# Odd tiles of the modulated norms finished by VectorE in two steps, with another order of work around the first projection and in the sparse attention

## What is computed

```python
def rms_norm(x, g):
    xf = x.astype(jnp.float32)
    y = xf * lax.rsqrt(jnp.mean(xf * xf, axis=-1, keepdims=True) + EPS)
    return (y * g.astype(jnp.float32)).astype(x.dtype)

def norm_modulate(h, g, shift, scale):
    return rms_norm(h, g) * (1 + scale) + shift
```

## Time and profile before

| | us |
|---|---|
| Three runs | 2070.64 (median), 2067.16, 2074.06 |
| The profiled execution, its own time | 2077.58 |
| Span of its instructions | 2075.7 |
| PE busy | 1947.7 (94%) |
| DVE busy | 1334.4 (64%) |
| ACT busy | 1073.5 (52%) |
| POOL busy | 280.0 (13%) |

### The profile page before, as it was taken

The page is one execution under the profiler, slowest core; times in us unless marked ns, Lnnn a source line. Parts: engine busy times, 40 slices in busy tenths (PEclk is TensorE's granted clock), DMA queues, the critical chain, the costliest instruction groups (busy, mean ns, idle before and its releaser), DMA issues.

```text
span 2075.7 us, 32710 instructions
## 1 busy us (share of the span) xinstructions
PE 1947.7 (94%) x13400; PEld 1659.5 (80%) x13400; DVE 1334.4 (64%) x2036; ACT 1073.5 (52%) x1744; POOL 280.0 (13%) x291
## 2 busy tenths in 40 slices
PE   6999889999999899899999889999988899999998
PEld 3675568888787785899998888999877688888886
DVE  2338545676545558677667556545666688888886
ACT  2346533333334466466555425444445577676774
POOL 1201123010100300332111412111101000000000
PEclk9999999999999899999999999999998999999998
DMA  8332443554222220245553113555542489889794
GB/s 320 127 137 103 163 175 109 183 183 183 110 85 90 88 102 21 89 177 183 203 184 141 43 38 121 200 183 203 202 165 72 177 326 341 324 319 349 303 346 164
DMA packets 52812, 364.81 MB, mean 176 GB/s; under 512 B 5936, under 2 KB 8240, under 8 KB 8880
## 3 DMA queue, kind: packets, MB, share of 16 engines
q1 hardware_dynamic: 50304, 359.68, 46.9%
q10 hardware_dynamic: 2352, 2.96, 0.5%
HBM read 361.57 MB, written 1.05 MB: 175 GB/s over the span
## 4 chain that ended last, share of the span: by engine, by line
PE 82%; DVE 8%; ACT 4%; issue 3%; POOL 2%; DMA 1%; SPq 0%; DVEq 0%; POOLq 0%; ACTq 0%
PE ps L77 22%; PE ps L78 21%; PE ps L79 21%; PE ps L74 15%; DVE WLO L91 3%; PE ps L82 2%; ACT R L85 2%; ACT WHI L85 1%; DVE SM L105 1%; POOL R L91 1%; DMA ring<-W 1%; DVE R L91 1%; POOL h L95 0%; DVE h L88 0%; DVE x L88 0%
## 5 line engine op out<-in xcount | busy, mean ns | idle before, releaser
L91 DVE TENSOR_TENSOR WLO<-ring,WHI 128x1024 fp32r<-128x1024 f32 x566 | 682.2, 1240 | 194.5 <-ACT WHI L85 193.9
L85 ACT ACTIVATE WHI<-ring 128x1024 fp32r<-128x1024 f32 x566 | 577.8, 1052 | 101.7 <-PE ps L79 98.0
L77 PE MATMUL ps<-HHI,WHI 128*128 128x256 f32 (+1 forms) x1584 | 514.4, 325 | 32.2 <-DVE HLO L88 18.0
L78 PE MATMUL ps<-HLO,WHI 128*128 128x256 f32 (+1 forms) x1648 | 526.1, 319 | 0.0
L79 PE MATMUL ps<-HHI,WLO 128*128 128x256 f32 (+1 forms) x1584 | 507.9, 321 | 0.0
L77 PEld LDWEIGHTS ps<-HHI,WHI 128*128 128x128 f32 x1584 | 305.1, 193 | 75.2 <-issue 29.0
L78 PEld LDWEIGHTS ps<-HLO,WHI 128*128 128x128 f32 x1648 | 316.1, 192 | 23.0
L79 PEld LDWEIGHTS ps<-HHI,WLO 128*128 128x128 f32 x1584 | 303.8, 192 | 24.3
L74 PE MATMUL ps<-R 64*64 64x64 f32 (+10 forms) x2448 | 192.7, 291 | 4.5 <-ACT R L85 2.5
L85 ACT ACTIVATE R<-ps,VEC 128x512 f32<-128x512 f32 (+1 forms) x106 | 69.3, 658 | 244.1 <-PE ps L79 242.0
L91 POOL TENSOR_TENSOR R<-R 128x256 f32<-128x256 f32 (+1 forms) x99 | 108.4, 1098 | 544.8 <-ACT R L85 543.6
(11 more groups left out here) (220 smaller groups left out, 2994.6 us busy)
## 6 DMA issues: line engine op xcount, KB each, us to landing
ring<-W SPq DMA_DIRECT2D x340, 1024.0 KB, 4.9
x<-xt SPq DMA_DIRECT2D x2, 1024.0 KB, 6.7
out<-x SPq DMA_DIRECT2D x2, 512.0 KB, 3.9
CR<-const_nsa ACTq DMA_DIRECT2D x1, 560.0 KB, 3.7
CR<-const_rw ACTq DMA_DIRECT2D x1, 448.0 KB, 3.4
CR<-const_gqa ACTq DMA_DIRECT2D x1, 320.0 KB, 10.3
CR<-const_mla ACTq DMA_DIRECT2D x1, 320.0 KB, 2.9
VEC<-vec ACTq DMA_DIRECT2D x1, 314.0 KB, 10.1
```

The source lines that it names most:

```text
L77: self.e.matmul(out, l[0], r[0], start=start, stop=False)
L78: self.e.matmul(out, l[0], r[1], start=False, stop=False)
L85: return self.e.activation(out, in_, func, **kw)
L91: return self.e.tensor_tensor(out, in0, in1, op)
```

## The change

In the modulated norms, for odd tiles, VectorE now writes x * rs into h, waits for that, and then finishes h * gain + shift in place. ScalarE's HHI of an odd tile is a plain copy and GpSimd has one subtraction left. Around norm 0 the two jobs, the weight units and the low part of tile 0 stand in another order: VectorE scales tile 0, subtracts unit 0, writes the low part of tile 0; unit 1 follows after tile 2, unit 2 after job 1, unit 3 after tile 5. TensorE does parts 0 to 2 of job 1 before k = 1, part 3 before k = 2 and the turn before k = 3. In the sparse attention ScalarE writes one WHI in each of rounds 2 to 5, between the exponentials and the copy, and the four subtractions for WLO are GpSimd's, by a new function. The diff in full:

```diff
--- before.py
+++ after.py
@@ -670,6 +670,14 @@
             e.tt(WLO[:, o:o + UNIT], src, WHI[:, o:o + UNIT], ALU.subtract).then_inc(
                 *did("w_lo", ("lo", u)))
 
+    def lo_units_pool(g, units):
+        for u in units:
+            c, col, _, _ = F.units[u]
+            o = (u % UNITS) * UNIT
+            g.wait_ge(*at("hi", u))
+            src = ring[:, (c % RING) * SLOT + col:(c % RING) * SLOT + col + UNIT]
+            g.tt(WLO[:, o:o + UNIT], src, WHI[:, o:o + UNIT], ALU.subtract).then_inc(*did("w_lo_pool", ("lo", u)))
+
     def split_of(p, o=0):
         return WHI[:, p.at:p.at + p.cn], WLO[:, p.at:p.at + p.cn]
 
@@ -873,7 +881,13 @@
         n = NORM[c]
         o, w = n["segs"][s]
         v.wait_ge(*at("rs", c))
-        v.stt(n["dst"](k)[:, o:o + w], n["src"](k)[:, o:o + w], n["gain"](k, s), bank("rs", c)[:, o:o + w],
+        d = n["dst"](k)[:, o:o + w]
+        if n["shift"] and not by_dve(c, k):
+            v.tt(d, n["src"](k)[:, o:o + w], bank("rs", c)[:, o:o + w], ALU.mult).then_inc(*did("normed"))
+            v.wait_ge(*last("normed"))
+            v.ts(d, d, n["gain"](k, s), n["shift"](k, s), ALU.mult, ALU.add).then_inc(*did("normed", ("nx", c, k, s)))
+            return
+        v.stt(d, n["src"](k)[:, o:o + w], n["gain"](k, s), bank("rs", c)[:, o:o + w],
               ALU.mult, ALU.mult).then_inc(*did("normed", ("nx", c, k, s)))
 
     def low_dve(v, c, k, s):
@@ -901,11 +915,14 @@
             if k < n["tiles"]:
                 for s in segs:
                     scale_dve(v, c, k, s)
-            if n["split"] and k >= 1 and by_dve(c, k - 1):
+            if n["split"] and k >= 1 and by_dve(c, k - 1) and (c or k > 1):
                 for s in segs:
                     low_dve(v, c, k - 1, s)
             if between:
                 between(k)
+            if (c, k) == (0, 0):
+                for s in segs:
+                    low_dve(v, c, 0, s)
 
     def apply_act(a, c, between=None):
         n = NORM[c]
@@ -913,7 +930,7 @@
             for s, (o, w) in enumerate(n["segs"]):
                 z = slice(n["t0"] + o, n["t0"] + o + w)
                 a.wait_ge(*at("nx", c, k, s))
-                if n["shift"]:
+                if n["shift"] and by_dve(c, k):
                     m = a.act(HHI[:, k, z], n["dst"](k)[:, o:o + w], ACT.Identity, bias=n["shift"](k, s))
                 else:
                     m = a.act(HHI[:, k, z], h[:, k, z], ACT.Copy)
@@ -929,10 +946,6 @@
             for s, (o, w) in enumerate(n["segs"]):
                 z = slice(n["t0"] + o, n["t0"] + o + w)
                 g.wait_ge(*at("nh", c, k, s))
-                if n["shift"]:
-                    d = n["dst"](k)[:, o:o + w]
-                    g.ts(d, d, n["shift"](k, s), None, ALU.add).then_inc(*did("pool_step"))
-                    g.wait_ge(*last("pool_step"))
                 g.tt(HLO[:, k, z], h[:, k, z], HHI[:, k, z], ALU.subtract).then_inc(*did("h_lo_pool", ("nl", c, k, s)))
 
 
@@ -1635,9 +1648,9 @@
     def gqa_pe(pe):
         st, steps = L["gqa_in"], L["ada0"]
         def second_job(k):
-            for s in {1: (0, 1), 2: (2,), 3: (3,)}.get(k, ()):
+            for s in {1: (0, 1, 2), 2: (3,)}.get(k, ()):
                 ada_part_pe(pe, L["ada_pe"][4 + s], 1, s)
-            if k == 4:
+            if k == 3:
                 ada_turn_pe(pe, 1)
                 give(bank_of["rs", 0])
 
@@ -3223,10 +3236,10 @@
 
     def nsa_act(a):
         for i in range(11):
-            if i == 6:
-                hi_units(a, L["o_out"].first)
             if 1 <= i < 8:
                 nsa_exp_act(a, i)
+            if 2 <= i < 6:
+                hi_units(a, L["o_out"].first[i - 2:i - 1])
             if 2 <= i < 10:
                 nsa_copy(a, i - 2, 1)
             if i >= 4 and i % 2 == 0:
@@ -3234,8 +3247,6 @@
 
     def nsa_dve(v):
         for i in range(1, 10):
-            if i == 7:
-                lo_units(v, L["o_out"].first)
             if i < 8:
                 nsa_max_dve(v, i)
             if 2 <= i <= 8:
@@ -3244,6 +3255,7 @@
                 nsa_copy(v, i - 2, 0)
 
     def nsa_pool(g):
+        lo_units_pool(g, L["o_out"].first)
         for f in range(4):
             g.wait_ge(*at("oh", f))
             g.tt(HLO[:, f, 0:256], h[:, f, 0:256], HHI[:, f, 0:256], ALU.subtract).then_inc(
@@ -3770,9 +3782,11 @@
         first_squares_act(a)
         root_act(a, 0)
         ada_row_act(a, 0, None)
-        hi_units(a, L["gqa_in"].first[0:2])
+        hi_units(a, L["gqa_in"].first[0:1])
 
         def second_job(k):
+            if k == 1:
+                hi_units(a, L["gqa_in"].first[1:2])
             if k == 3:
                 ada_row_act(a, 1, 0)
                 hi_units(a, L["gqa_in"].first[2:4])
@@ -3832,12 +3846,14 @@
         ada_job_dve(v, 0)
 
         def second_job(k):
+            if k in (0, 2):
+                lo_units(v, L["gqa_in"].first[k // 2:k // 2 + 1])
             if k == 3:
-                v.wait_ge(*at("mod0", 0, 0))
                 ada_job_dve(v, 1)
-                lo_units(v, L["gqa_in"].first[2:4])
+                lo_units(v, L["gqa_in"].first[2:3])
                 v.wait_ge(*at("mod", 0, 1))
-        lo_units(v, L["gqa_in"].first[0:2])
+            if k == 5:
+                lo_units(v, L["gqa_in"].first[3:4])
         apply_dve(v, 0, [("mod", 0, 0)], second_job)
         gqa_dve(v)
```

## The result

The changed kernel took 2061.74 us (median; 2054.73 to 2068.00) beside 2072.53 us (2065.68 to 2081.55) for the kernel before: a ratio of 0.9947, 95% interval 0.9935 to 0.9959, some 10.8 us less (8.5 to 13.5 by the interval). A second comparison (`b1_after`) gave 0.9962 (0.9948 to 0.9976), 7.9 us less (5.0 to 10.8). The forecast was 12.9 us less, 2057.7: within the first interval and outside the second.

The account below looks back on a forecast made before the run. TensorE, 82% of the chain of waits, bounds the kernel, so only its standstills can shrink: 5.1 + 0.8 + 3.4 - 0.2 + 3.8 = 12.9 us, from 2070.64 to 2057.7; range 2050 to 2066.

Parts of the forecast that it names:

- Norm 0: First projection: TensorE starts tile 0 1.8 us earlier and resumes at tile 4 5.1 us earlier, 1.8 included; bounds 2.5 to 7.6.
- rival (b): Chunk 8's load late by 2.6 us at norm 0, VectorE held in the attention: 5.9 less gained, 2063.6; chance 0.13.
- rival (a): Short waits at tile 4 and in the attention leave TensorE's clock high: 17 us gained, 2054; chance 0.13.
- The two steps: Odd tiles' finish on VectorE: 0.73 us a piece, 0.34 more for each of 28, 9.5 us of VectorE in all.
- GpSimd's two subtractions of tile 1, 0.73 each, can start at 305.3 at the latest, behind VectorE's unit: Norm 1: so TensorE goes on at once after k = 0, at 309.1, where before it went on at 309.88.
- norm 1: TensorE starts 0.7 us later but no longer waits at tile 1: gain 0.8 us, bounds 0 and 1.1.
- Norm 2: Start slips 0.65 us, the pause at tile 1 goes and the clock rises earlier: gain 3.4 us, bounds 1.1 and 4.5.
- as the step said: Norm 2: without the pause TensorE's clock should rise some 5.6 us after its start, up by about 708.
- Sparse attention: Four WLO leave VectorE's path, 5.0 us, less 1.2 of holds by GpSimd: gain 3.8 us, bounds 0 and 6.5.
- Rival (c): Attention: each GpSimd WLO holds VectorE for its whole 2.35 us, 15.3 lost there, 2077 in all; chance 0.06.
- Norm 5: One segment, no wait on GpSimd; the two steps cost a loss of 0.2 us, bounds 0.5 lost and none.
- Rival (d): GpSimd's additions were hidden, TensorE stood for something else at tile 1 and odd tiles only grow: 2063.2; chance 0.08.

Follow-up runs that it names:

- b1_after: The changed kernel once more, unchanged, in a second comparison with the kernel before: ratio 0.9962 (0.9948 to 0.9976), median 2064.81 us.
- a5_turn_late: The changed kernel with the turn of job 1 before k = 4 again, all else new: ratio 0.9972 to the kernel before, median 2067.34 us.
- n4_pool_waits: The changed kernel with one wait more: GpSimd's subtraction of an odd tile waits for VectorE's low part of the even tile before; 0.9932 to the kernel before.
- a7_best: The changed kernel with attention WLO on VectorE in idle places, tile 0's low part before tile 1's scaling, GpSimd's odd-tile subtraction waiting for the even low part: 0.9944.
- n2_first: The kernel before with only the new order around the first projection (norm 0): ratio 0.9976 (0.9964 to 0.9988), 5.0 us faster.
- b2_best: The same kernel as a7_best, on another chip beside the changed kernel: ratio 0.9939 (0.9918 to 0.9959) to the kernel before, 2059.06 us.

## Why the prediction was right, and where its terms were off

The path was right: which waits of TensorE shrink, and why. The measured time lies in the range, and the 12.0 us of the stretches near the 12.9. Part of that nearness is luck, as told at norm 0, norm 2 and the attention, and the second comparison's 7.9 us is well short of it.

**Norm 0 (5.1 forecast, 5.5 in the profile).** From the gains on, tile 0 starts at 3.10 us and not 4.89: 1.8, as worked out. Tile 4 starts at 24.17 and not 29.48: 5.3. Two errors cancel in it, which is luck. The clock rose some 4 us after TensorE's start and not the assumed 6 (the stretch 36 to 40 has a granted clock of 1.00, where the earlier trace rows have 0.79), so the turn came 17.4 us after the gains and not 18.7. And VectorE's way from the sums (44.59) to the last low part took a us more than forecast, for the hold. Hence a wait of 2.89 and not 1.9. `a5_turn_late` puts k = 3 behind the turn at 2.1 to 2.5 us. Chunk 8 was in time, so rival (b)'s first half did not occur. Nor, in this profile, did rival (a): behind tile 4 the clock was low from 50 to 54, and in the attention's last transposes (1565.68) too.

**The two steps (0.73 a piece forecast, 0.77 measured).** The page's groups, shapes apart (count, busy us, mean ns):

```profile
L88 DVE SCALAR_TENSOR_TENSOR HLO<-h,MOD,HHI 128x256 fp32r<-128x256 f32 x28 | 23.0, 853 | 0.0
L96 DVE TENSOR_SCALAR h<-h,GS,MOD 128x256 f32<-128x256 f32 x28 | 11.6, 414 | 1.0
L91 DVE TENSOR_TENSOR h<-x,ps 128x256 f32<-128x256 f32 x28 | 11.6, 413 | 0.0
```

There are 28 more, as predicted, at 414 ns and not 350: with two operands from tiles it is dearer than the one-operand row. The first row shows what the sum missed: HLO at a mean of 853 ns, where one alone takes 0.48.

**The step that failed: "GpSimd's two subtractions of tile 1, 0.73 each, can start at 305.3 at the latest, behind VectorE's unit".** They were looked at as something that TensorE waits for. But without the addition and with a plain copy, they become ready just as VectorE starts the low part of tile 0, the one piece on TensorE's path, and hold it for 0.93 us (`n4_pool_waits`). The prediction weighed the shared port only in the attention. The start of norm 1 was to slip by 0.7 us and slipped by 1.7. So norm 1 gave 0.1 for 0.8. Norm 2's stretch gave 2.6 for 3.4, and only 1.3 of them at the norm: its start slipped 1.6 and not 0.65, 1.3 us went to the two small brackets, and at the end of TensorE's block of tiles the lead over the kernel before had grown by 1.3. Its clock rose as the step said, earlier:

```profile
700.00:704.00 4.00, 4.00 (x23) 3.67 (x22) 3.96 (x7) 0.79 (x3) 1.71 (x2) 0.73 0.00 0
704.00:708.00 4.00, 3.11 (x21) 2.54 (x21) 3.93 (x9) 1.66 (x5) 1.72 (x2) 1.00 0.72 262
```

(columns as in the earlier trace rows): full from about 702.2, 4.8 us after the start, and the pause of 0.89 at 707 did not lower it. Of the rest of norm 2's row, 1.2 us came some 45 us later, behind a wait of 1.89 us that both kernels have: the clock fell in the kernel before (first row) and not in the changed one (second row).

```profile
768.00:772.00 4.00, 4.00 (x12) 3.10 (x12) 2.49 (x8) 3.92 (x7) 0.00 (x0) 0.57 0.72 262
760.00:764.00 4.00, 3.62 (x16) 3.00 (x17) 3.09 (x9) 3.89 (x8) 0.00 (x0) 1.00 0.58 215
```

No step of the prediction covers that; it did not fall in `b1_after` either, and fell in other traces of either finish.

**Sparse attention (3.8 forecast).** GpSimd's 2.35 us was met to the digit. VectorE was held in three rounds, 1.0, 0.8 and 0.1 us over the 0.17 of the earlier trace rows, 1.9 in all where 1.2 was forecast. The last bracket is 2.43, not the 1.3 expected; yet the stretch fell by 4.2 us in this pair of profiles and by 3.6 in the means of four and six. Of the pair's 4.2 us, some are the clock's: in `b1_after`, the same code as the changed kernel, the stretch took 51.72 us and not 53.97, with the same wait of 2.43 us followed by transposes at the high clock.

```profile
1573.50 1.09 PE L82 MATMUL ps<-C,R 128*128 128x128 f32 x8 [2.43 <-DVE R L91]
```

In time it isn't resolved: with and without this part the ratios differ by -0.0001 (alone), +0.0007 (beside the new order of the first projection) and -0.0014 or +0.0001 (in the whole, by its two comparisons), each uncertain by about 0.002. Whether the 3.6 us reach the end stays open. Rival (c) is excluded: a hold lasts what is left of GpSimd's instruction, not all of it.

**Norm 5** lost some 0.4 us, where 0.2 was forecast: the lead of the changed kernel's trace falls from 8.7 us at its first scaling to 8.3 us behind its tiles.

**Do the parts add?** Alone they gave 4 us (+1.2, -5.0, -0.2); together they gave 8 to 11. The difference is just clear of noise by the first comparison and not by the second. The prediction did not need it, since each term was worked out with the other edits in place. Rival (d), that the additions were hidden, holds only where VectorE is the later one: at norm 0 they were hidden in the old order and are a wait of 3.06 us in the new one.

## What to carry to other kernels

When an instruction of GpSimd becomes ready earlier, look at what VectorE does at that moment: the gain of the one can be a hold of the other, just in front of the engine that bounds. Two edits that look at the same wait must be priced together: alone, the finish in two steps made both waits of norm 0 longer (6.92 us), and the new order alone left one of 3.06 us; together there are 3.41 us at tile 0, 2.89 at tile 4 and none at tile 5. In time the finish was worth nothing alone and 3 to 7.5 us beside the new order, each figure uncertain by some 4 us. And an independent piece of the bounding engine's work (k = 3 here) is best placed behind the hand-over that others need, not ahead of it. Last, a gain read in one pair of profiles holds the luck of the clock and of the pace too: compare a second profile of the same code first.

## What the runs showed of the hardware

GpSimd's subtraction of a 128x1024 float32 tile takes 2.35 us, where VectorE needs 1.23. While it runs, a 128x4 tensor_scalar of VectorE took up to 1.21 us and not 0.17, always to the end of GpSimd's instruction (1545.97 + 2.36 = 1548.33, and 1547.17 + 1.19 = 1548.36). The Trainium skill ("SBUF — State Buffer", section "SBUF: two separate sides") tells of a port pair that GpSimd shares with some of VectorE's instructions, and of an exclusive lock on it for a whole instruction. These ends agree with it.

At a granted clock of 1.00, without a gap, TensorE has two paces. In the same stretch of the second feed-forward net it did 214 matmuls in 24 us in some executions and 206 in others (0.112 and 0.1165 us each), and the same kernel showed both. Windows of 24 or 25 us of the kernel before, of the changed kernel, and of the changed kernel once more:

```profile
900.00:925.00 25.00, 25.00 (x215) 25.00 (x214) 19.51 (x27) 15.95 (x27) 6.42 (x9) 1.00 0.55 192
```
```profile
892.00:916.00 24.00, 24.00 (x214) 24.00 (x214) 19.34 (x27) 16.30 (x27) 6.71 (x9) 1.00 0.56 194
```
```profile
892.00:916.00 24.00, 24.00 (x206) 24.00 (x205) 18.56 (x26) 15.49 (x27) 5.97 (x8) 1.00 0.51 187
```

The stretch from norm 5 to the attention, the same work in all but for norm 5's start, took 653.0 to 662.1 us in the profiles. The window's pace does not order them alone (`a7_best` had 215 matmuls in its window and 658.8 us, `n2_first` 206 and 653.4), so the pace is not fixed over an execution, or something else adds to it; that stays open. The changed kernel itself took 653.31 and 662.09 us in its two profiles: one pair can differ by 9 us there for no reason in the code, so spans were compared stretch by stretch.

And a wait of the same length did not always lower the clock. The 1.89 us behind norm 2, the 2.01 us in norm 1's stretch and the 2.43 us in the attention are told above; the first two were worth 1.2 and 1.5 us. In the attention 0.97 us were followed by eight matmuls in 1.86 us before; in `b2_best` 0.98 us were followed by the same eight at the high clock:

```profile
1551.13 1.09 PE L82 MATMUL ps<-C,R 128*128 128x128 f32 x8 [0.98 <-DVE R L91]
```
